# Relative-bias tables and group merge of the dilated attention layer: tables read during the projections, merge and output product in one stage

## The reference

```python
DIL_GROUPS = ((128, 1), (512, 4), (2048, 16))        # window, dilation; 8 heads of 64 in each group

def dilated_attention(xn, w_qkv, w_o, rel_bias):
    qkv = (xn @ w_qkv).reshape(B, S, 3, G, Hg, dh)
    for g, (window, dilation) in enumerate(DIL_GROUPS):
        o, lse = strided_window_attention(qkv[:, :, 0, g], qkv[:, :, 1, g], qkv[:, :, 2, g],
                                          dilation, window // dilation, rel_bias[:, g * Hg:(g + 1) * Hg])
        outs.append(o); lses.append(lse)
    wts = jax.nn.softmax(jnp.stack(lses), axis=0)
    o = jnp.einsum('gbshd,gbsh->bshd', outs, wts).reshape(B, S, Hg * dh)
    return o @ w_o
```

## Time and profile before

| | |
|---|---|
| median of 3 runs | 2292.49 us |
| profiled execution | 2290.96 us |
| its span, first to last instruction | 2289.2 us |
| PE busy | 2077.6 us, 91% of the span |
| DVE, ACT, POOL busy | 1181.4, 870.1, 342.5 us |
| mean granted TensorE clock | 0.964 of full speed |
| DMA | 163.65 MB, mean 71 GB/s |

### The profile page before, as it was taken

One profiled execution on the slowest core, in us unless ns is written; L12 is line 12 of the kernel. 1 busy time (PEld: TensorE's weight loads), 2 busy tenths in 40 slices (PEclk: granted clock), 3 DMA queues, 4 the chain that ended last, 5 costly groups with the idle time before them and its releaser, 6 DMA issues. The chain is left out here.

```text
span 2289.2 us, 28407 instructions
## 1 busy us (share of the span) xinstructions
PE 2077.6 (91%) x11540; PEld 1630.2 (71%) x11540; DVE 1181.4 (52%) x1435; ACT 870.1 (38%) x1249; POOL 342.5 (15%) x322
## 2 busy tenths in 40 slices
PE   8999888799988889887999999989997859999996
PEld 4777866477786668643778888868895746888885
DVE  4445653444565353243487457454324657854753
ACT  4236432533644241354344234332122625432431
POOL 1200632120063220133110000120000032000002
PEclk9999999899999999999999999999999889999998
DMA  5221011222101122100222322222221012223221
GB/s 207 74 74 56 3 74 37 94 73 74 56 3 74 37 92 92 37 1 1 83 83 87 105 94 105 88 74 102 101 92 37 1 37 74 92 89 105 105 82 62
DMA packets 27167, 163.65 MB, mean 71 GB/s; under 512 B 2755, under 2 KB 6267, under 8 KB 11420
## 3 DMA queue, kind: packets, MB, share of 16 engines
q1 hardware_dynamic: 27036, 161.81, 19.9%
HBM read 155.47 MB, written 6.33 MB: 71 GB/s over the span
## 5 line engine op out<-in xcount | busy, mean ns | idle before, releaser
L251 PE MATMUL psum<-inputs_high,weights_high 128*128 128x512 f32 x928 | 376.7, 406 | 15.6 <-DVE inputs_low L232 8.7
L253 PE MATMUL psum<-inputs_high,weights_low 128*128 128x512 f32 x928 | 362.0, 390 | 0.0
L252 PE MATMUL psum<-inputs_low,weights_high 128*128 128x512 f32 x928 | 361.7, 390 | 0.0
L1843 PE MATMUL psum<-inputs_high,weights_high 128*128 128x512 f32 x704 | 276.4, 393 | 7.9 <-DVE inputs_low L1981 7.9
L237 DVE TENSOR_TENSOR weights_low<-weights_raw,weights_high 128x2048 fp32r<-128x2048 f32 x72 | 168.6, 2342 | 209.2 <-ACT weights_high L226 209.1
L1844 PE MATMUL psum<-inputs_low,weights_high 128*128 128x512 f32 x704 | 274.7, 390 | 0.0
L1845 PE MATMUL psum<-inputs_high,weights_low 128*128 128x512 f32 x704 | 274.4, 390 | 0.0
L226 ACT CAST weights_high<-weights_raw 128x2048 fp32r<-128x2048 f32 x72 | 136.7, 1899 | 230.8 <-PE psum L253 191.5
L251 PEld LDWEIGHTS psum<-inputs_high,weights_high 128*128 128x128 f32 x928 | 174.1, 188 | 70.4 <-DVE inputs_low L232 13.5
L252 PEld LDWEIGHTS psum<-inputs_low,weights_high 128*128 128x128 f32 x928 | 174.3, 188 | 37.8 <-issue 4.3
L253 PEld LDWEIGHTS psum<-inputs_high,weights_low 128*128 128x128 f32 x928 | 174.2, 188 | 37.2
(11 more groups left out here) (334 smaller groups left out, 3335.9 us busy)
## 6 DMA issues: line engine op xcount, KB each, us to landing
weights_raw<-w_stream SPq DMA_DIRECT2D x116, 1024.0 KB, 4.8
weights_raw<-w_down SPq DMA_DIRECT2D x32, 704.0 KB, 4.1
residual_parked<-residual SPq DMA_DIRECT2D x2, 2048.0 KB, 10.0
residual_back<-residual_parked SPq DMA_DIRECT2D x2, 2048.0 KB, 7.8
residual<-x_t SPq DMA_DIRECT2D x1, 2048.0 KB, 7.7
out_t<-residual SPq DMA_DIRECT2D x8, 256.0 KB, 2.0
constants<-consts SPq DMA_DIRECT2D x1, 1537.5 KB, 11.5
table_backward<-bias_rows SPq DMA_DIRECT2D x1, 1024.0 KB, 5.7
```

Of the source, the lines that this page charges most:

```text
L251: pe.matmul(out, hi, self.ahi[:, k], start=start and b == 0, stop=False)
L252: pe.matmul(out, hi, self.alo[:, k], start=False, stop=False)
L253: mm = pe.matmul(out, lo, self.ahi[:, k], start=False, stop=stop and b == blocks - 1)
L1843: pe.matmul(out, wh, hi, start=start, stop=False)
```

## The change

1. *Bias tables.* `start` is as before up to one more scratch buffer, `bias_by_row`. During `stick_attention`, which had no SP stream, three DMAs from DRAM to DRAM write each row of `bias_rows` 128 times (384, 256 and 256 values wide in the three groups). During `dilated_projections`, after chunk 6, three DMAs read a skewed view of these copies (a row stride one less than the row length), which comes out in forward order, straight into the tables; the table of group 0 lies in `num[:, 4:8]`. The stage `bias_tables` is gone. The SP stream waits there for the updated residual and issues the loads one by one, in the old order.
2. *Merge and output product* are one stage, `dilated_output`. PE sorts group 0's maxima and sums into the classes with columns of the identity (16 matmuls), so that the weights are made on 128 partitions with 32 to 96 elements. Sixteen matmuls with a spread matrix bring group 0's weights back to token order. DVE scales the 12 tiles instead of POOL, and PE adds the groups: 48 plain matmuls by the identity, of 128 columns, accumulate in PSUM banks 0 to 3; for groups 1 and 2 they write every fourth column. ACT and DVE read the high and low inputs from PSUM. `wake` is gone, and the eight output tiles use eight banks.
3. *Constants.* The flip matrix is gone and the spread matrix is new. Masks used only by the hybrid layers are a table of their own (`hcon`) that is given back after these layers; one more DMA at the start, and `late` is waited for at 48 instead of 32.

```diff
 def stick_attention(nc, k, qk, v, out):
         with nc.Block() as block:
+            @block.sync
+            def _(sp):
+                for g, w in enumerate(BIAS_WIDTH):
+                    rows = bass.AP(k.bias_rows.tensor, g * DIL_HEADS * 384, [[384, DIL_HEADS], [0, P], [1, w]])
+                    sp.dma_start(k.bias_by_row[g], rows).then_inc(s.bias_repeated, 16)
+                sp.wait_ge(s.bias_repeated, 16 * DIL_GROUPS)
...
-def bias_tables(nc, k, tables):
...
 def dilated_projections(nc, k, m, inv, squares, q, kk, v, tables):
             def _(sp):
-                st.load(sp, s)
+                for c in range(2, DIL_CHUNKS + 2):
+                    sp.wait_ge(s.split, c - 1)
...
+                    if c == 6:
+                        sp.wait_ge(s.new_x, KD)
+                        for g, w in enumerate(BIAS_WIDTH):
+                            width = 2 * P if g == 0 else P
+                            skewed = bass.AP(k.bias_by_row[g].tensor, P - 1, [[w - 1, P], [P * w, DIL_HEADS], [1, width]])
+                            sp.dma_start(tables[g], skewed).then_inc(s.table, 16)
+                sp.wait_ge(s.table, 16 * DIL_GROUPS)
...
-def dilated_merge(nc, k, num, top, total, out):
+def dilated_output(nc, k, num, stats, out, ahead):
...
+    order = [TT * g + t for g in (1, 2, 0) for t in range(TT)]
...
             @block.tensor
             def _(pe):
+                for c in range(rate):
+                    for t in range(TT):
+                        mm = pe.matmul(ps[32 * t:32 * t + 32, 4, c * 16:c * 16 + 16], by_class(ident, rate)[:, c],
+                                       stats[:, t].rearrange("p y h -> p (y h)"), start=True, stop=True)
+                mm.then_inc(s.classed, 1)
+                pe.wait_ge(s.weight, 1)
+                for t in range(TT):
+                    rows = slice(32 * t, 32 * t + 32)
+                    for c in range(rate):
+                        mm = pe.matmul(ps[:, 4 + t, 0:DIL_HEADS], spread[rows, c], e[rows, 0, c], start=c == 0,
+                                       stop=c == rate - 1)
+                    mm.then_inc(s.natural, 1)
+                for m, n in enumerate(order):
+                    g, t = n // TT, n % TT
+                    pe.wait_ge(s.scaled, m + 1)
+                    for f in range(TT):
+                        dst = ps[:, f, t * P:(t + 1) * P] if g == 0 else by_class(ps[:, f], rate)[:, t]
+                        mm = pe.matmul(dst, num[:, n, f * P:(f + 1) * P], ident, start=m == 0, stop=m == len(order) - 1,
+                                       skip_group_check=True)
+                        if m == len(order) - 1:
+                            mm.then_inc(s.merged, 1)
+                for c in range(DIL_OUT_CHUNKS):
+                    pe.wait_ge(s.split, c + 1)
...
             @block.scalar
             def _(act):
+                st.high(act, s, 0, 0)
+                act.wait_ge(s.step, 5)
+                act.activation(e[:], e[:], ACT.Exp, scale=-1.0).then_inc(s.exp, 1)
+                st.high(act, s, 1, 1)
+                for f in range(TT):
+                    act.wait_ge(s.merged, f + 1)
+                    act.copy(k.ahi[:, f], ps[:, f]).then_inc(s.in_hi, 1)
...
-            dilated_projections(nc, k, m, inv, squares, q, kk, v)
...
+            dilated_projections(nc, k, m, inv, squares, q, kk, v, tables)
+            dilated_scores(nc, k, q, kk, v, tables, num, top, total)
+        dilated_output(nc, k, num, stats, m, (k.w_stream, AT_UP[1], CHUNK))
```

More of the change, by code:

```diff
@@ L375, in _ @@
                 st.load(sp, s)
-                sp.wait_ge(k.late, 32)
+                sp.wait_ge(k.late, 48)
             @block.tensor
@@ L2044, in _, with dilated_projections @@
                             dve.tensor_tensor(m[:, j], m[:, j], ps[:, q % banks], ALU.add).then_inc(s.freed, 1)
-def bias_tables(nc, k, tables):
[L2051 to L2073, removed]
-            @block.vector
-            def _(dve):
-                for m, (g, n) in enumerate(parts):
-                    dve.wait_ge(s.flipped, m + 1)
-                    dve.tensor_copy(columns_of(tables[g], n), ps[:, m]).then_inc(s.table, 1)
 def by_class(x, rate):
     return x.rearrange("p (l c) -> p c l", c=rate)
-def dilated_projections(nc, k, m, inv, squares, q, kk, v):
+def dilated_projections(nc, k, m, inv, squares, q, kk, v, tables):
     ps, con, x = k.ps, k.con, k.x
@@ L2441, in _ @@
+                act.wait_ge(s.freed, KD)
+                act.activation(k.last_square, out[:, KD - 1], ACT.Square).then_inc(s.square, 1)
+            @block.gpsimd
+            def _(pool):
+                add_squares(pool, s, sq, k.total, KD - 1)
             @block.vector
@@ L2477, in _ @@
-            @block.gpsimd
-            def _(pool):
-                pool.wait_ge(s.column, 1)
-                for n in range(G * TT):
+                dve.wait_ge(s.classed, 1)
+                step(dve.tensor_copy(first[:].rearrange("p t y h -> p (t y h)"), ps[:, 4, 0:TT * 2 * DIL_HEADS]))
+                step(dve.tensor_tensor(low[:], rest[:, 0, :, 0], rest[:, 1, :, 0], ALU.min))
+                step(dve.tensor_tensor(low[:], low[:], first[:, :, 0], ALU.min))
+                step(dve.tensor_tensor(e[:, 0], first[:, :, 0], low[:], ALU.subtract))
@@ L2481, in _ @@
                     x = num[:, n].rearrange("p (h e) -> p h e", h=DIL_HEADS)
-                    pool.tensor_tensor(x, x, col[:, n].unsqueeze(2).to_broadcast([P, DIL_HEADS, 64]), ALU.mult) \
+                    dve.tensor_tensor(x, x, col.unsqueeze(2).to_broadcast([P, DIL_HEADS, 64]), ALU.mult) \
                         .then_inc(s.scaled, 1)
+                st.low(dve, s, 0, 0)
+                st.low(dve, s, 1, 1)
+                st.input_low(dve, s)
+                for tile in range(KD):
+                    dve.wait_ge(s.made, tile + 1)
+                    dve.tensor_copy(out[:, tile], ps[:, (tile + 4) % 8]).then_inc(s.freed, 1)
```

181 lines of the change are left out of this document (84 added, 97 removed).

## The result

The changed kernel takes 2258.26 us (median of 4 runs, 2255.96 to 2260.76) against 2292.05 us for the kernel before (4 runs): the ratio is 0.9851, its 95% interval 0.9833 to 0.9868, and the change saves 33.8 us. Predicted were 2256.0 us, with a range of 2244 to 2271. Timed again, it gave 2259.95 against 2293.59 (ratio 0.9855, 0.9840 to 0.9871).

A forecast was written before the change was run, and what follows sets the result against it. PE, busy 91% of the span, was taken as the limit, with gains only where it stands or works slowly. Savings of 16.8 (table stage) and 18.2 us (merge and output) gave 2290.96 - 35.0 = 2256.0 us, range 2244 to 2271.

The forecast's parts named there:

- Table stage: Between projections and scores: first scores start 0.33 us after the projections' last ACT instruction, minus 16.8 us.
- The covers: Row copies (some 29 us), table reads and the added constants table lie beside other work and cost nothing.
- Merge and output: From the end of the scores to the feed-forward: 47.2 us instead of 65.4, minus 18.2.
- sorting: Group 0 into classes, 16 f32 matmuls on PE: 2.6 us, bounds 1.3 to 6.9.
- spreading: Group 0's weights back to token order, 16 matmuls on PE: 3.9 us, bounds 3.9 to 6.9.
- adding: 48 plain f32 matmuls on PE, half clock for 4 us, then full: 12.8 us, bounds 10.7 to 22.1.
- DVE as cover: From the weights on, DVE's scaling and low parts take 12.1 us, less than PE's 16.7, so PE sets the pace.
- Cold PE: Rival: clock never rises in the adding; the new stage takes 59.5 us, saving only 5.9; 2268.3 us; chance 0.14.
- Warm throughout: Rival: sorting 1.3, adding 10.7, weights 2, scores tail 3.5 shorter; 7.9 us less, 2248.1; chance 0.12.
- Strided writes: Rival: writing every fourth column of a bank halves the speed of 32 adding matmuls; 7.0 us more, 2263.0; chance 0.04.
- repeated rows: Rival: row copies during stick-breaking attention outlast some 130 us hidden; at 200 us the kernel takes 2326; chance 0.03.
- The feed-forward begins at another clock and gives the gain back: Sign that the forecast is wrong, in the feed-forward behind the new stage; no size given.

The follow-up runs named there:

- rotated: The changed kernel with the loops of the 16 spreading matmuls exchanged, so neighbours use different groups of 32 partitions; 2253.64 us.
- tail_warm: The changed kernel plus unused matmuls: two where PE waits for the weights, one and two in the last two turns of the scores; 2253.74 us (1 run).
- contiguous: The changed kernel with groups 1 and 2 added into 128 neighbouring columns instead of every fourth, so token order is lost; 2262.18 us (1 run).
- repeats3: The changed kernel with the bias rows written out three times instead of once, the attention stage's end waiting for all; 2259.42 us.

## Why the prediction was right

- *Table stage, -16.8.* Exactly as read: the first score 0.30 us after the last `dilated_v` (0.33 foreseen). The covers held: the copies, priced at 29 us, take 20 in a stretch of 161, and the table reads ended no wait.
- *Merge and output, 47.2.* Measured 46.6. That the sum is only 0.6 off is in part luck: the terms missed by 4.0 us in all, 2.3 of them downward and 1.7 upward.

| term | predicted | measured | from |
|---|---|---|---|
| sorting | 2.6 | 0.7 | L2408 |
| weights | 3.0 | 3.2 | 1815.73 to 1818.97 |
| spreading | 3.9 | 4.5 | L2415 |
| adding | 12.8 | 13.7 | L2423 |
| first inputs | 1.2 | 0.8 | before L258 |
| output product | 23.7 | 23.7 | 1837.93 to 1861.64 |

- *Sorting* is the term mis-sized: the 0.68 us for 32 records lie below the lower bound of 1.3. The rows that I priced it from had 64 or 128 weight columns and 64 moving ones, with neighbours on two different halves of the partitions in the 0.08 row. Here there are 32 weight columns and 16 moving ones, and neighbours write to four different groups of 32 partitions. `rotated` showed for the spreading what changing groups are worth; how much of the sorting's price is due to that, and how much to the fewer columns, no run separates. The Trainium skill (TensorEngine Tiling (Array Packing), Key Properties) says that different tiles can load weights and multiply in parallel; the traces of the spreading agree (0.06 against 0.14 us a record).
- *Adding.* The mechanism was right, half clock first and full later, and its two prices too (0.42 and 0.22 measured, 0.46 and 0.22 foreseen). The clock rose 5.7 us into the series where I had put 4. My argument that records of 64 columns stay cold and lines of 128 do not was weak: the earlier trace rows also shows 16 records of 64 columns in 1.90 us at full clock, and here records of 128 columns ran at 0.50 for those 5.7 us. The fourfold price of a plain f32 product against a transpose, which the Trainium skill gives (TensorE: Matmul & The Clock Gate, Terms), would have made the full-clock price 0.47; the measurement is 0.22.
- *DVE as cover.* Low parts done at 1830.9, the last addition at 1837.1: 6 us of room.
- *Rivals.* "Cold PE" needed the clock low to the end of the adding, and it rose 8 us before. "Warm throughout" did not happen by itself, but fillers produced most of it: its 7.9 us compare with the 6.9 of `tail_warm`. (Its shorter tail should have been 6.92 - 32 x 0.12 = 3.1, not 3.5; measured with fillers, 3.25. "Cold PE", in turn, left the sorting at 2.6 where its own 0.22 a record gives 7.) "Strided writes" is out by `contiguous`, "repeated rows" by `repeats3`.
- *Left out.* "The feed-forward begins at another clock and gives the gain back" was named as a danger and not priced. The feed-forward itself did not change (376.96 us from its first cast to the last norm, and 376.95); the norm's four matmuls took 1.7 us more, and what follows them 0.6 less. The two parts alone gave 16.8 + 18.8 = 35.6 us; with the 1.1 us taken off, 34.5, against my 35.0 and the 33.8 between the medians.

## What to carry to other kernels

A chain of short steps between barriers, visible as a stretch in which no engine is busy throughout, can be priced row by row; here the whole came out well although single terms did not, in part because their misses cancelled. Small per-head steps on 8 partitions and 512 to 1536 elements are the ones to look for: on 128 partitions and 32 to 96 elements they took 3.9 us with their hand-offs instead of 22.1. Small matmuls that use only part of the array should be ordered so that neighbours use different parts. After a change that shortens a stage, look at where PE stands in the stages behind it: the clock's falls may land on other instructions, and two or three matmuls with unused results in a pause that is there anyway may win that back.

## What the hardware showed that I had not expected

- Small f32 matmuls on different groups of 32 partitions overlap: 32 records in 1.89 us against 4.51 at the same granted clock. Another 32, with 32 weight columns and changing groups of partitions written, took 0.68.
- The granted clock stayed at 0.50 through ten microseconds in which PE never paused (1819 to 1829); two fillers in the pause ahead of them brought the rise forward by 10 us, the changed order of the spreading by 3.4.
- Matmuls that write every fourth column of a PSUM bank run as fast as those that write neighbouring ones (13.67 and 13.44 us for 96 records, the 0.2 being the clock's).
- DRAM to DRAM copies with rows of 1 to 1.5 KB, each source row read 128 times, moved 192 GB/s in the mean at a DMA share of 0.5. Their outermost dimension has 8 entries (heads). The Trainium skill (DMA: Bandwidth & Descriptors, Rules for kernel authors) says that an outermost dimension below 16 keeps a DMA to as many engines; half of 16 agrees with the share of 0.5, though no run here changed that dimension.
- POOL's scaling of a 128 x 512 tile takes 1.04 us, and took 3.1 in the two cases in which DVE subtracted a 128 x 2048 chunk beside it. What in the two instructions collides was not tested.
- Executions of one kernel fall into a few patterns, told apart by where the granted clock is at 0.50: the scores took 81.4 or 85.2 us with the same instructions, and the stretch from the 43rd to the 55th cast 296.8, 299.6 or 300.2.
